# Retention scores as three products of rounded parts, and finer waits at three places, in a hybrid attention, retention and PEER block

## What is computed

```python
h = rms_norm(x, mix_norm)
aq, ak, av, rq, rk, rv, rg, ga, gr = split(h @ w_in)
# attention: 8 heads of 128, window of two chunks of 64, softmax with sinks
# retention: 4 heads, q and k of width 256, v of width 512
rq, rk = apply_rope(rq), apply_rope(rk)
inner = einsum('bcnhd,bcmhd->bchnm', rq, rk) * decay
y_ret = group_norm(inner @ rv + state part) * silu(rg) @ w_o_ret
x = x + (sigmoid(ga) * y_att + sigmoid(gr) * y_ret) @ w_out
x = x + peer(rms_norm(x))                # 128 x 128 experts, top 16 per head
x = x + sigmoid(rms_norm(x) @ w_pg) * (p @ w_pe)
return rms_norm(x)
```

## Time and profile before

| | us |
|---|---|
| median of 3 runs | 1984.89 (1984.79 to 1986.66) |
| the profiled execution | 1985.89 |
| its span in the trace | 1984.1 |
| TensorE busy | 1958.0 (99%) |
| VectorE busy | 1366.9 (69%) |
| GpSimd busy | 1233.6 (62%) |
| ScalarE busy | 806.2 (41%) |

### The profile page before, as it was taken

One profiled execution on the slowest core, in us unless ns is written; L12 is line 12 of the kernel. 1 busy time (PEld: TensorE's weight loads), 2 busy tenths in 40 slices (PEclk: granted clock), 3 DMA queues, 4 the chain that ended last, 5 costly groups with the idle time before them and its releaser, 6 DMA issues.

```text
span 1984.1 us, 27327 instructions
## 1 busy us (share of the span) xinstructions
PE 1958.0 (99%) x10232; PEld 1725.7 (87%) x10232; DVE 1366.9 (69%) x2287; ACT 806.2 (41%) x1272; POOL 1233.6 (62%) x686
## 2 busy tenths in 40 slices
PE   7999999999999999999999999999999999999998
PEld 6888888888888788999999999999888888888887
DVE  6433333342741479998968888861999899999976
ACT  5222222232553333433346666654433333333352
POOL 4343434352234433899996767766998898988842
PEclk9999999999999999999999999999999999999999
DMA  5222222233223232899997999998999999999931
GB/s 198 85 91 85 91 85 85 85 117 112 80 75 96 96 120 83 322 335 352 366 358 268 387 375 362 370 387 277 360 372 360 365 360 353 367 367 363 359 104 43
DMA packets 171953, 471.93 MB, mean 238 GB/s; under 512 B 13776, under 2 KB 62928, under 8 KB 170064
## 3 DMA queue, kind: packets, MB, share of 16 engines
q1 hardware_dynamic: 58032, 209.04, 30.2%
q0 software_dynamic: 41472, 151.01, 20.7%
q10 hardware_dynamic: 72352, 110.64, 15.5%
HBM read 413.49 MB, written 54.53 MB: 236 GB/s over the span
## 4 chain that ended last, share of the span: by engine, by line
PE 94%; DVE 2%; ACT 1%; DMA 1%; issue 0%; ACTq 0%; POOL 0%; POOLq 0%; SPq 0%; DVEq 0%
PE bank L932 29%; PE bank L934 28%; PE bank L933 28%; PE bank L1185 4%; PE bank L1047 1%; PE bank L1130 1%; DMA raw<-weights 1%; PE bank L1115 1%; PE bank L1091 0%; PE bank L1101 0%; DVE bank L1364 0%; DMA xT<-x_cols 0%; ACTq L793 0%; PE bank L1016 0%; PE bank L1138 0%
## 5 line engine op out<-in xcount | busy, mean ns | idle before, releaser
L493 POOL TENSOR_TENSOR w_lo<-raw,w_hi 128x1024 fp32r<-128x1024 f32 x390 | 936.9, 2411 | 655.6 <-ACT w_hi L550 652.1
L932 PE MATMUL bank<-h_hi,w_hi 128*128 128x352 f32 (+2 forms) x1560 | 549.2, 352 | 1.4 <-DVE h_lo L1537 1.4
L934 PE MATMUL bank<-h_hi,w_lo 128*128 128x352 f32 (+2 forms) x1560 | 538.1, 345 | 0.0
L550 ACT ACTIVATE w_hi<-raw 128x1024 fp32r<-128x1024 f32 x390 | 407.6, 1054 | 320.0 <-DMA raw<-weights 271.6
L933 PE MATMUL bank<-h_lo,w_hi 128*128 128x352 f32 (+2 forms) x1560 | 537.2, 344 | 0.0
L932 PEld LDWEIGHTS bank<-h_hi,w_hi 128*128 128x128 f32 x1560 | 293.8, 188 | 21.2 <-DVE h_lo L1537 1.8
L933 PEld LDWEIGHTS bank<-h_lo,w_hi 128*128 128x128 f32 x1560 | 294.7, 189 | 19.7
L934 PEld LDWEIGHTS bank<-h_hi,w_lo 128*128 128x128 f32 x1560 | 293.1, 188 | 20.7
L1753 DVE TENSOR_TENSOR b_lo<-scr,b_hi 128x384 fp32r<-128x384 f32 x128 | 267.7, 2092 | 47.5 <-ACT b_hi L846 47.4
L932 PE MATMUL bank<-w_hi,b_hi 128*128 128x512 f32 x768 | 298.9, 389 | 0.1
L934 PE MATMUL bank<-w_hi,b_lo 128*128 128x512 f32 x768 | 298.8, 389 | 0.0
(11 more groups left out here) (227 smaller groups left out, 2707.5 us busy)
## 6 DMA issues: line engine op xcount, KB each, us to landing
raw<-weights SPq DMA_DIRECT2D x390, 512.0 KB, 6.1
act_scratch<-scr ACTq DMA_DIRECT2D x64, 384.0 KB, 7.0
gate_scratch<-scr ACTq DMA_DIRECT2D x12, 2048.0 KB, 13.1
scr<-gate_scratch ACTq DMA_DIRECT2D x22, 768.0 KB, 11.8
scr<-act_scratch ACTq DMA_DIRECT2D x22, 768.0 KB, 17.4
xT<-gate_scratch ACTq DMA_DIRECT2D x10, 768.0 KB, 9.8
xT<-act_scratch ACTq DMA_DIRECT2D x10, 768.0 KB, 14.5
scr<-scr ACTq DMA_DIRECT2D x20, 128.0 KB, 3.8
```

The source lines that it names most:

```text
L493: return nc.gpsimd.tensor_tensor(w_lo[:, s, :], raw[:, s, :], w_hi[:, s, :].bitcast(F32), ALU.subtract)
L550: nc.scalar.activation(w_hi[:, u_mod, :], raw[:, u_mod, :], ACT.Copy).then_inc(hi_done, 1)
L932: nc.tensor.matmul(out, a_hi, c_hi, start=first, stop=False)
L934: return nc.tensor.matmul(out, a_lo, c_hi, start=False, stop=last)
```

## The change

The turned q and k of a head are split by DVE (`split_pair`) into a rounded and a rest part, each 128x1024, in a new buffer `qk_parts` that lies where `more` lies later. The scores of 512, 384 and 256 columns use these parts with `mm3`; that of 128 columns stays as it was. In the first head both splits follow the turn of k; in the others q is split before k is turned, and k between the two pairs of `transposed_lower`. The signal `rot_ready` now comes with the split. Besides: `p_ready` counts tiles, not heads; ACT's rounding of weights at the merge stops at four units further and goes on later; and the transposes of `y_tok` are put in an order in which those of tiles emptied earlier come first.

```diff
+        with nc.sbuf_tensor("qk_parts", [P, 4, UW], F32R) as qk_parts:
+            pass
         more = sb("more", [P, 4, UW])
...
-                run_ahead(UNIT[("ga", KT - 1)] + 4 + m)
+                run_ahead(UNIT[("ga", KT - 1)] + 4 + min(m, 4))
...
-                        ins = nc.tensor.matmul(bank[:, 2 + j, 0:S - P * j], r_k[:, c, P * j:P * j + P],
-                                               r_q[:, c, P * j:S], start=c == 0, stop=c == 1)
+                        out, a, q = bank[:, 2 + j, 0:S - P * j], slice(P * j, P * j + P), slice(P * j, S)
+                        if j < TT - 1:
+                            ins = mm3(out, r_k_hi[:, c, a], r_k_lo[:, c, a], r_q_hi[:, c, q], r_q_lo[:, c, q],
+                                      c == 0, c == 1)
+                        else:
+                            ins = nc.tensor.matmul(out, r_k[:, c, a], r_q[:, c, q], start=c == 0, stop=c == 1)
...
-                    pe.wait_ge(p_ready, h + 1)
                     for t in range(TT):
+                        pe.wait_ge(p_ready, TT * h + t + 1)
...
+            pe.wait_ge(y_act_ready, TT - 1)
+            pe.wait_ge(y_dve_ready, TT - 1)
+            for k in range(4):
+                for t in (TDT, 0, 1):
+                    turn_y(k, t)
             pe.wait_ge(y_act_ready, TT)
+            for k in range(4):
+                turn_y(k, TDT - 1).then_inc(yT_done, 1)
             pe.wait_ge(y_dve_ready, TT)
-            for k in range(KT):
+            for k in range(4, KT):
...
-                ve.sem_inc(rot_ready, 1)
+
+            def split_pair(z, hi, lo):
+
+                step(nc.vector.tensor_copy(hi, z))
+                mark(tt(lo, z, hi.bitcast(F32), ALU.subtract), rot_ready)
...
             end_pair(0, ("rk", 1), r_k)
+            split_pair(r_q, r_q_hi, r_q_lo)
+            split_pair(r_k, r_k_hi, r_k_lo)
...
-                    for kind, dst in (("rq", r_q), ("rk", r_k)):
-                        begin_pair(i, (kind, 2 * i), dst)
-                        end_pair(i, (kind, 2 * i + 1), dst)
-                    transposed_lower(i - 1, range(4))
+                    begin_pair(i, ("rq", 2 * i), r_q)
+                    end_pair(i, ("rq", 2 * i + 1), r_q)
+                    split_pair(r_q, r_q_hi, r_q_lo)
+                    begin_pair(i, ("rk", 2 * i), r_k)
+                    end_pair(i, ("rk", 2 * i + 1), r_k)
+                    transposed_lower(i - 1, (0, 1))
+                    split_pair(r_k, r_k_hi, r_k_lo)
+                    transposed_lower(i - 1, (2, 3))
...
-                    together([lambda t=t: ts(a_s[:, h % 2, t, :], a_s[:, h % 2, t, :], rden[:, t:t + 1], None, ALU.mult)
-                              for t in range(TT)])
-                    ve.sem_inc(p_ready, 1)
+                    for t in range(TT):
+                        ts(a_s[:, h % 2, t, :], a_s[:, h % 2, t, :], rden[:, t:t + 1], None, ALU.mult).then_inc(p_ready, 1)
```

More of the change, by code:

```diff
@@ L259, in block_program @@
         r_k = cut3(8704, 2, S)
+        r_q_hi, r_q_lo, r_k_hi, r_k_lo = (qk_parts[:, n, :].rearrange("p (c t) -> p c t", c=2) for n in range(4))
         r_v_hi, r_v_lo = b_hi[:, TT:, :], b_lo[:, TT:, :]
@@ L1251, in _, with turn_y @@
             up_turn(NKEY // STEP - 1)
+            def turn_y(k, t):
+                return nc.tensor.transpose(bank[:, YT_BANKS[k], P * t:P * t + P], y_tok[:, t, P * k:P * k + P], ident)
+            pe.wait_ge(y_act_ready, TT - 1)
[3 more added lines that the diff above has]
+                    turn_y(k, t)
             pe.wait_ge(y_act_ready, TT)
+            for k in range(4):
+                turn_y(k, TDT - 1).then_inc(yT_done, 1)
             pe.wait_ge(y_dve_ready, TT)
-            for k in range(KT):
+            for k in range(4, KT):
                 if k >= 6:
@@ L1258, in _ @@
                 for t in range(TT):
-                    ins = nc.tensor.transpose(bank[:, YT_BANKS[k], P * t:P * t + P], y_tok[:, t, P * k:P * k + P], ident)
+                    ins = turn_y(k, t)
                 ins.then_inc(yT_done, 1)
```

## The result

The changed kernel takes **1989.37 us** (median of 17 runs, 1986.98 to 1991.44) where the kernel before takes 1985.60 (17 runs, 1984.48 to 1989.08): a ratio of **1.0016**, with a 95% interval of 1.0009 to 1.0022. So it is slower, by 0.16%, which is under the 0.2% that counts as no change here. The forecast was 1988.3, the range 1983.5 to 1991.4.

The account below looks back on a forecast made before the run. TensorE, with 94% of the chain of waits and busy 99% of the span, was taken as the bound. Saved 6.1 us, lost 9.5, net +3.4 on the median 1984.89: forecast 1988.3 us, range 1983.5 to 1991.4.

Parts of the forecast that it names:

- Scores: TensorE's scores in each head: 4.23 us falls to about 3.5, saving 2.9 us in four heads.
- The first head's wait: TensorE before tile 2 of v in the first head: a new wait of 7.8 us, bounds 4.0 and 8.5.
- The walk: First head: step-by-step times of VectorE's splits taking turns with GpSimd, from 49.4 us until TensorE goes on at 58.1.
- rival A: First head: the four split instructions run in 4.0 us beside GpSimd, without taking turns; net -0.4, 1984.5 us; chance 0.12.
- rival B: First head: the bank isn't what counts, so only the gains are left; 1978.8 us; chance 0.08.
- The clock: TensorE behind the first head's new wait: a low clock adds 1.7 us, bounds 0 and 3.4.
- Rival D: Behind the first head's wait the clock stays low twice as long, 1.7 us more; 1990.0 us; chance 0.12.
- Later heads: At k's split r_v_lo ends at 127.3 us, TensorE needs the bank at 128.75; 1.4 us of cover, no cost.
- Rival C: Three later heads wait 1.0 us each if GpSimd gets one unit more in between; total 1991.3 us; chance 0.13.
- Merge: TensorE's wait for ACT's last merged tile goes entirely: 1.5 us saved, bounds 1.2 and 1.5.
- probabilities: TensorE's wait of 2.0 us before the transposes of probabilities: 0.7 us saved, bounds 0.4 and 1.0.
- expert output: TensorE's wait before the transposes of the expert output is filled by 12 transposes: 1.0 us saved, bounds 0.3 and 1.0.

## Why the prediction held, point by point

**Scores: right.** Forecast 3.5 us a head, measured 3.50 and 3.51. 384 columns were put half way between 256 and 512; measured 0.173 us apart, forecast 0.17. The gain of 2.9 us came in full.

**The first head's wait: right in mechanism and size.** Forecast 7.8 us, measured 7.6. The walk took its price from one held instruction elsewhere, and its steps came out like this:

| ends at (us) | forecast | measured |
|---|---|---|
| cast of q | 51.9 | 52.0 |
| subtraction of q | 55.2 | 55.3 |
| cast of k | 56.0 | 56.0 |
| subtraction of k | 57.2 | 57.3 |
| first `r_v_lo` | 57.9 | 58.0 |
| TensorE goes on | 58.1 | 58.1 |

The run with GpSimd idle (3.95) settles against rival A, which had 4.0 us for the changed kernel itself. Moving the splits settles against rival B: TensorE really stood behind that bank. Rival A could have been weighed better beforehand: the forecast left open whether a cast, with its one input, is held, and the trace of before shows one that is, 1.91 us for 256 columns where 512 take 0.43 with GpSimd idle:

```profile
69.54 1.91 DVE L1474 CAST b_hi<-scr 128x256 fp32r<-128x256 f32 x1
```

**The clock: the term that was mis-sized.** I took half of the 3.4 us stretch of the earlier trace rows because half the rate loses half the time, and gave 0 and 3.4 as bounds. Measured: 2.8. The rule of half is right, but the stretch was longer: low from 53.9 to 64.1, of which TensorE worked through 6.0. The shorter wait's 3.4 us was the wrong row to scale from, though the 2.8 lies within the bounds. Rival D, with 1.7 us more, was nearer on this term: its 3.4 against 2.8 measured. As a net, its +5.1 lies further from the +3.8 measured than the forecast's +3.4. So the forecast's +3.4 for the change should have been +4.5 by its own terms with this one put right.

**Later heads: right.** `r_v_lo` was to end at 127.3. Less the 9.8 us by which all is later, it ended at 127.27, with 1.5 us to spare. Rival C is out for the changed kernel, and the run with both splits there shows where it would begin.

**Merge, probabilities, expert output: right.** Forecast 1.5, 0.7 and 1.0, measured 1.65, 0.70 and 1.03. The merge gave 0.15 more than the bound that I had set above it, 1.5. The kernel with only these waits gives 2.34 for the first two together and 1.03 for the third.

**The sum.** Net forecast +3.4, found +4.0 between the traces for the terms of the change, and +3.8 between medians of 17 runs. The forecast's median (1988.3) lies 1.1 us under that measured, of which 0.7 is the reference: the median before was 1984.89 in the three runs shown and 1985.60 in seventeen. The other 0.4 is less than the 1.1 that the clock had too little, in part because the wait came out 0.2 and the merge 0.15 better than forecast. That the total came so near is partly luck, and the medians can't tell more: single executions of one kernel differ by up to 4.6 us, and the interval of the ratio is 2.6 us wide.

## What to carry to other kernels

When elementwise work is added to an engine that shares a resource with another, place it by who stands behind it: these four instructions cost nothing two instructions later, in a gap, and 10.3 us where they stood. Read the price of each off an instruction that was already held in the trace, not off its free duration, and walk the two engines' timelines against each other. Add the clock to every new idle time of TensorE, since here it added 1.7 to 2.8 us to each of the waits from 4 to 8 us.

## What the runs showed that was not expected

**The clock's price hardly followed the wait's length.** Behind extra waits of 3.95, 6.1 and 7.66 us in the first head the granted clock was 0.50 for 14, 10 and 14 products of TensorE, by the starts of its products, which cost 2.7, 2.0 and 2.8 us. Behind three waits of 4.74 us in one execution, one in each later head, it cost 2.3, 2.1 and 1.7 us. What sets the price in each wasn't tried.

**Short waits: sometimes.** Behind one wait of 2.0 us, before the probabilities, the clock fell in the trace of one kernel and not in that of before. The low stretch at about 23 us stands in the traces of before, of the changed kernel, of the waits alone and of GpSimd idle, and in none of the other six, though no edit touches that place. TensorE's wait at about 21 us, just ahead of it, was 1.4 to 1.5 us in the four and 0.3 to 1.1 in the six. A single trace doesn't tell whether such a stretch belongs to a kernel. The mean granted clock of every run does: of the 53 runs of the kernel before beside the experiments, the 15 at 0.999 have a median of 1984.9 us, the 26 at 0.998 one of 1986.1, the 11 at 0.997 one of 1987.4, and the one at 0.996 took 1988.6. A stretch of 3.4 us at half the clock lowers the mean by 0.0009. So such stretches seem to come and go from run to run of one kernel, and with them much of the spread of its times; only the traced runs show where they lie.

**A cast with one input is held like a subtraction with two.** 0.69 us free, 2.39, 2.27 and 2.77 held. In these traces the turns go one by one: where both engines have work waiting, a VectorE instruction of this kind lets one unit of GpSimd pass before it.
